# A decoder layer's two FFNs: where the combinations of x for the half-size products are made, and four plain blocks in the first FFN

## The chip, the cores and the metric

The kernel runs on one core of one Trainium2 chip. The metric is the device time of one execution in microseconds; the median of several runs is given. TensorE (PE) multiplies matrices, VectorE (DVE) and ScalarE (ACT) do elementwise work, GpSimd (POOL) a little of it, and SyncE's queue (SP) issues the loads of weights.

## The reference, cut to what matters

The input x is 512 tokens by 1024 features, float32. The layer is a SwiGLU FFN of half weight, a token mixer, and another FFN of half weight:

```python
x = x + 0.5 * swiglu(rmsnorm(x, ffn1_norm), ffn1_w_gate, ffn1_w_up, ffn1_w_down)
h = rmsnorm(x, mix_norm); proj = h @ w_in
...
x = x + jnp.concatenate([hm, hp], axis=-1) @ w_out
x = x + 0.5 * swiglu(rmsnorm(x, ffn2_norm), ffn2_w_gate, ffn2_w_up, ffn2_w_down)
return rmsnorm(x, final_norm)
```

with `swiglu(h, g, u, d) = (silu(h @ g) * (h @ u)) @ d` and an inner width of 2816, which is 22 blocks of 128 features. mlstm heads (`hm`) and a causal pooling (`hp`) stand in the mixer; they play no part here.

## The kernel before, in words

Everything lies transposed: features on the 128 partitions, the 512 tokens along the free axis. x is 8 tiles of 128 x 512 (k = 0 to 7). A float32 product is made of three passes: each operand is split into a high part (`_hi`, rounded, made by ScalarE) and a low part (`_lo`, operand minus high part, made by VectorE), and TensorE does hi*hi, hi*lo and lo*hi. The weights come in units of 128 x 1024, which SP loads into two slots `raw`; ScalarE and VectorE split them into four slots `w_hi`, `w_lo`. A slot of `raw` is free for the next load once its low part is made (`lo_made`).

An FFN (`ffn_up`) has 22 blocks of inner features. Each needs a gate column and an up column.

- A **plain block** uses two weight units, 24 matmuls of 512 tokens each (L341 to L343), with x times its gain in `plain_x`. Gate and up land in two banks of `ps`; VectorE multiplies the gate by `rinv` (`plain_gate`, L1266), ScalarE takes the silu (L797), VectorE multiplies (`plain_product`, L1271), ScalarE copies the high part to `act_hi` (`act_high`, L802), VectorE makes the low part (`act_low`, L1262).
- A **half-size block** computes the 2 x 2 block product (gate and up against the two halves of the tokens, with the two halves of the inner dimension) by seven products instead of eight, each of 12 matmuls of 256 tokens (`product`, L426 to L428), 84 in all. Its seven weight factors are sums of four 128 x 512 blocks, made by VectorE (`sum_1` L1231, `sum_3` L1237, `sum_2` L1241, `sum_4` L1248), then split by ScalarE (L793) and VectorE (L1256). The results are put together by ScalarE's copies of P1, P5 and U2 (L815, L819, L830) and VectorE's corners (L1277 to L1300). The products stand in the order 1, 5, 6, 2, 7 with 3 and 4 of the block before among them (`period`). Product 6 waits for the copy of P1.

The half-size products also need **combinations of x**: for each k below 4, from the tile k and the tile k+4, each cut in halves of 256 tokens, the four terms t1, t3, t2, t4 (`x_terms`: L1215, L1216, L1218, L1220). t1 is split into `xg_hi`/`xg_lo` (L772, L1222), the other three together into `xe_hi`/`xe_lo` (L774, L1225). ScalarE first copies tile k times its gain to `rinv`, used as scratch here (L769), and before all that the part of x that is used as it is (`own_block`, L780, L781). Product 1 of the first block waits for all of these (`te_made`).

`rinv`, the reciprocal root of the mean square of every token, spread over the partitions, is made thus: TensorE sums columns (`mean_columns`, L383), VectorE computes the root (`inverse_rms`, L1190 and L1178 to L1183), TensorE spreads it over the partitions (`replicate`, L375) at a fixed place in the matmuls of the fourth unit, VectorE copies it (`take_rinv`, L1199).

Before the change each FFN has 2 plain blocks (`PLAIN`) and then 20 half-size ones (`NS`). Every engine works a list in fixed order; what lies ahead in one's list delays all behind it. VectorE's list at the start of an FFN is:

```python
x_terms(0); x_terms(1); inverse_rms(stage); x_terms(2); x_terms(3)
sum_1(0); sum_3(0, True); sum_2(0); lo_of(1, 0, 0); lo_of(5, 0, 0)
take_rinv(stage); plain_gate(0); lo_of(6, 0, 0); sum_4(0, True); plain_product(0)
```

(one line each there). The first FFN follows the loading of x; the second follows the mixer's output projection (`out_blocks(WO_UNIT, 1, 2, ...)`), in which, for each of 8 columns d, TensorE does one unit, VectorE adds the result to x[d] (L1382), splits a weight unit (L1148), makes the low part of x[d] times its gain (L1154) and adds the square (L1164), and ScalarE splits a unit (L743), makes the high part (L753) and squares (L760).

Of the kernel before, what the change touches and what calls it, by code (L numbers as in the profile page):

```python
# [30 lines left out]
T = 512  # L31
# [18 lines left out]
PLAIN = 2  # L50
NS = FB - PLAIN
UPP1 = 0
DN1 = UPP1 + 2 * PLAIN
# [8 lines left out]
DN2 = UPP2 + 2 * PLAIN  # L62
N_UNITS = DN2 + DN_UNITS * KD
SUP = (N_UNITS, N_UNITS + 2 * NS)
AFTER = (DN1, DN2)
N_ROWS = N_UNITS + 4 * NS
# [32 lines left out]
def build_layer(nc, weights, pool_w, x_t, vecs, consts, out):  # L99
    ctx = ExitStack()  # L100
    with ctx:
# [51 lines left out]
        tt = work[:, 0:2].rearrange("p a n -> p (a n)")  # L153
# [5 lines left out]
        zeros = sums[:, 3]  # L159
# [101 lines left out]
        def _(sp):  # L261
# [28 lines left out]
            def strassen_blocks(p):  # L290
                q = AFTER[p]
                sp.wait_ge(lo_made, q - 1)
                load_block(p, 0, 0)
                load_block(p, 0, 1)
                sp.wait_ge(lo_made, q)
                load_block(p, 0, 2)
                load_block(p, 0, 3)
                with sp.Fori(1, NS) as s:
                    sp.wait_ge(s_made[3], s + p * NS)
                    load_block(p, s, 2)  # L300
                    sp.wait_ge(f_lo[1], s + p * NS)
                    load_block(p, s, 0)
                    sp.wait_ge(f_lo[4], s + p * NS)
                    load_block(p, s, 3)
                    sp.wait_ge(f_lo[2], s + p * NS)
                    load_block(p, s, 1)
                sp.wait_ge(f_lo[1], (p + 1) * NS)
                sp.wait_ge(f_lo[2], (p + 1) * NS)
                load(q, q)
                sp.wait_ge(s_made[3], (p + 1) * NS)  # L310
                sp.wait_ge(f_lo[4], (p + 1) * NS)
                load(q + 1, q + 1)
# [10 lines left out]

            strassen_blocks(0)
# [14 lines left out]
        def _(pe):  # L339
# [52 lines left out]
            def ffn_up(base, p, stage, mean_at, rep_at):  # L392

                def plain(f):
# [13 lines left out]
                    for i in range(2):  # L408
                        n = base + 2 * f + i
                        column_block(n, n, ps[:, 2 * f + i], before(2 * f + i), plain=True)  # L410
# [8 lines left out]
                def product(i, s, par, acc, first=False):  # L419

                    pe.wait_ge(f_lo[i], s + (p * NS + 1))
# [9 lines left out]
                def last_two(s, par, steps):  # L431

                    if 3 in steps:
                        pe.wait_ge(p5_copied, s + (p * NS + 1))
                        product(3, s, par, ps_c[par])
                    if 4 in steps:
                        pe.wait_ge(c22_made, s + (p * NS + 1))
                        product(4, s, par, ps_b[par])

                def period(s, par, early=False, head=False):  # L440
                    if head:
                        pe.wait_ge(b11_made, 2 * (p + 1))
                        pe.wait_ge(te_made, 2 * KH * (p + 1))
                    if not early:
                        pe.wait_ge(prod_made, s + (p * FB + PLAIN - 1))
                    product(1, s, par, ps_b[par], True)
                    if not early:
                        pe.wait_ge(c12_made, s + (p * NS - 1))
# [3 lines left out]
                    pe.wait_ge(p1_copied, s + (p * NS + 1))  # L452
# [5 lines left out]
                    else:  # L458
                        pe.wait_ge(c11_made, s + p * NS)
                    product(2, s, par, ps_a, True)  # L460
                    pe.wait_ge(u2_copied, s + (p * NS + 1))
                    product(7, s, par, ps_b[par])

                for f in range(PLAIN):
# [3 lines left out]
                with pe.Fori(1, NS // 2) as it:  # L468
                    period(it * 2, 0)
                    period(it * 2 + 1, 1)  # L470
                last_two(NS - 1, 1, (3, 4))
# [263 lines left out]
        def _(act):  # L735
# [25 lines left out]

            def ffn_up(base, p, stage):
                q = AFTER[p]

                def x_terms(k):

                    if k > 0:
                        act.wait_ge(t_step, 4 * (p * KH + k))
                    act.activation(rinv[:], x[:, k], ACT.Copy, scale=scalar_of(V_GAIN + stage * KD + k)  # L769
                                   ).then_inc(b1_made, 1)  # L770
                    act.wait_ge(t_step, 4 * (p * KH + k) + 1)
                    act.activation(xg_hi[:, k, HALF:T], tt[:, 0:HALF], ACT.Copy).then_inc(t_hi_made, 1)  # L772
                    act.wait_ge(t_step, 4 * (p * KH + k) + 4)
                    act.activation(xe_hi[:, :, k], tt[:, HALF:].rearrange("p (a n) -> p a n", n=HALF), ACT.Copy  # L774
                                   ).then_inc(t_hi_made, 1)

                def own_block():

                    act.wait_ge(xg_made, KD * stage + KH)
                    act.activation(xg_hi[:, 0:KH, 0:HALF], f32(act_hi[:, XP:FB, 0:HALF]), ACT.Copy).then_inc(b11_made, 1)  # L780
                    act.activation(xg_lo[:, 0:KH, 0:HALF], f32(act_lo[:, XP:FB, 0:HALF]), ACT.Copy).then_inc(b11_made, 1)  # L781

                def hi_of(i, s, par):

                    if i in (5, 6, 3, 7):
                        j = {5: 1, 6: 2, 7: 3, 3: 4}[i]
                        act.wait_ge(s_made[j], s + (p * NS + 1))
                        src = s_sum[j]
                    else:
                        j = {1: 0, 2: 1, 4: 3}[i]  # L790
                        act.wait_ge(blk_in[j], s * 16 + 16 * (p * NS + 1))
# [12 lines left out]
                def split_after(j):  # L804

                    for i in ((1, 5), (6, 2), (7, 3), (4,))[j]:
                        act.wait_ge(p_done[i], (p + 1) * NS)
# [4 lines left out]
                def iteration(s, par, head=False, tail=False):  # L812

                    act.wait_ge(p_done[1], s + (p * NS + 1))
# [3 lines left out]
                    act.wait_ge(p_done[5], s + (p * NS + 1))  # L818
# [7 lines left out]
                    else:  # L826
                        act.wait_ge(p_done[3], s + p * NS)
                    hi_of(3, s, par)
                    act.wait_ge(p_done[6], s + (p * NS + 1))
# [3 lines left out]
                    if not head:  # L833
                        silu(s + (PLAIN - 1))
                    if not tail:
                        if head:
                            act.wait_ge(unit_used, q)
                        else:
                            act.wait_ge(p_done[4], s + p * NS)
                        hi_of(4, s + 1, 1 - par)  # L840
                    if not head:
                        act_high(s + (PLAIN - 1))
                    if tail:
                        split_after(1)
                    else:
                        act.wait_ge(p_done[2], s + (p * NS + 1))
                        hi_of(2, s + 1, 1 - par)
                        act.wait_ge(p_done[7], s + (p * NS + 1))
# [8 lines left out]
                silu(0)  # L857
                act.wait_ge(unit_used, q - 2)
                hi_of(6, 0, 0)
                act_high(0)  # L860
# [3 lines left out]
                silu(1)  # L864
                act.wait_ge(unit_used, q)
                hi_of(4, 0, 0)
                act_high(1)
                iteration(0, 0, head=True)
                iteration(1, 1)
                with act.Fori(1, NS // 2 - 1) as it:  # L870
                    iteration(it * 2, 0)
                    iteration(it * 2 + 1, 1)
                iteration(NS - 2, 0)
                iteration(NS - 1, 1, tail=True)
# [5 lines left out]
            def out_blocks(base, per, stage):  # L880

                for d in range(KD):
# [8 lines left out]
                    square_x(d, stage)  # L891
                    if stage == 3:
# [252 lines left out]
        def _(dve):  # L1145
# [55 lines left out]

            def ffn_up(base, p, stage):
                q = AFTER[p]

                def x_terms(k):

                    at = 4 * (p * KH + k)
                    far = scalar_of(V_GAIN + stage * KD + KH + k)
                    b11, b12 = rinv[:, 0:HALF], rinv[:, HALF:T]
                    x21, x22 = x[:, KH + k, 0:HALF], x[:, KH + k, HALF:T]  # L1210
                    t1, t3, t2, t4 = (tt[:, i * HALF:(i + 1) * HALF] for i in range(4))
                    dve.wait_ge(b1_made, p * KH + k + 1)
                    if k > 0:
                        dve.wait_ge(te_made, 2 * (p * KH + k))
                    dve.tensor_tensor(t1, b12, b11, ALU.subtract).then_inc(t_step, 1)  # L1215
                    dve.scalar_tensor_tensor(t3, x22, far, b12, ALU.mult, ALU.subtract).then_inc(t_step, 1)  # L1216
                    dve.wait_ge(t_step, at + 2)
                    dve.tensor_tensor(t2, t3, b11, ALU.add).then_inc(t_step, 1)  # L1218
                    dve.wait_ge(t_step, at + 3)
                    dve.scalar_tensor_tensor(t4, x21, far, t2, ALU.mult, ALU.subtract).then_inc(t_step, 1)  # L1220
                    dve.wait_ge(t_hi_made, 2 * (p * KH + k) + 1)
# [534 lines left out]
```

## Time and profile before

| | |
|---|---|
| median of 3 runs | 958.43 us (958.25 to 959.22) |
| the profiled execution, device time | 960.42 us |
| its span in the trace | 958.6 us |
| mean granted TensorE clock | 0.976 of full |
| TensorE / VectorE / ScalarE / GpSimd busy | 95% / 73% / 48% / 6% |
| loaded from memory | 89.14 MB, 95 GB/s over the span |

The span is the trace's own clock from the first to the last instruction; the device time of the same execution is 1.8 us more. A busy share says little of what bounds a stage: an engine's row in the timeline names, in brackets, how long it idled before an instruction and what released it. Where a row is followed by the next start of the same engine, the difference is what the instruction costs in a full list; it can be less than its duration, since neighbours overlap a little.

### The profile page before, as it was taken

Reading aid. Unit: us, or ns where it says so; the run is one execution under the profiler, and the core shown is the slowest. Engines: PE = TensorE matmul, PEld = TensorE weight load, DVE = VectorE, ACT = ScalarE, POOL = GpSimd, SP = SyncE. Lnnn points to the kernel's source line nnn. Section 1 sums busy time; section 2 is a strip of 40 time slices with the busy share of each in tenths; the row PEclk is TensorE's granted clock in tenths of the full one; section 3 lists DMA queues with packets and bytes.
Section 4 is the critical chain, followed back from the end, with each engine's and each line's share of the span. In section 5 each row is a group of like instructions: output and inputs, shape, how many; then the busy total and the mean of one; then the engine's idle time right before and its main releaser. Section 6 shows DMA issues by size and latency. Waiting matters only on the chain.

```text
span 958.6 us, 15901 instructions
## 1 busy us (share of the span) xinstructions
PE 909.7 (95%) x5672; PEld 819.9 (86%) x5672; DVE 702.1 (73%) x1213; ACT 459.2 (48%) x766; POOL 58.2 (6%) x75
## 2 busy tenths in 40 slices
PE   8769999999999999999989999699999999999995
PEld 5569999999988888888878788599999999888885
DVE  7879999999744343578887676799999998534334
ACT  5455666666523232444772344556666665323220
POOL 4000000000000000000443300000000000000002
PEclk9879999999999999999999999799999999999997
DMA  5123332332343233222211131133323332432312
GB/s 187 61 84 98 106 108 92 109 109 91 107 143 102 97 109 110 75 81 86 67 67 44 66 114 62 44 111 109 109 89 108 109 98 99 132 102 99 107 44 88
DMA packets 40005, 91.73 MB, mean 96 GB/s; under 512 B 4401, under 2 KB 7729, under 8 KB 39969
## 3 DMA queue, kind: packets, MB, share of 16 engines
q1 hardware_dynamic: 39792, 90.79, 29.0%
q8 instruction: 22, 0.36, 0.2%
q0 software_dynamic: 176, 0.46, 0.1%
q14 instruction: 15, 0.11, 0.0%
HBM read 89.14 MB, written 2.10 MB: 95 GB/s over the span
## 4 chain that ended last, share of the span: by engine, by line
PE 42%; DVE 32%; DMA 12%; issue 8%; ACT 5%; DVEq 1%; SPq 0%; ACTq 0%
PE ps L341 14%; PE ps L342 14%; PE ps L343 13%; DMA raw<-weights 11%; DVE w_lo L1256 11%; DVE sums L1248 3%; DVE sums L1237 3%; DVE work L1280 3%; DVE work L1286 1%; DVE work L1288 1%; DVE work L1277 1%; ACT xe_hi L774 1%; DVE sums L1241 1%; ACT w_hi L743 1%; DVE xe_lo L1225 1%
## 5 line engine op out<-in xcount | busy, mean ns | idle before, releaser
L1148 DVE TENSOR_TENSOR w_lo<-raw,w_hi 128x1024 fp32r<-128x1024 f32 x83 | 103.6, 1249 | 127.5 <-ACT w_hi L743 121.3
L426 PE MATMUL ps<-xg_hi,w_hi 128*128 128x256 f32 x640 | 185.5, 290 | 5.1 <-DVE w_lo L1256 3.1
L341 PE MATMUL ps<-act_hi,w_hi 128*128 128x512 f32 (+1 forms) x470 | 180.7, 385 | 3.5 <-DVE act_lo L1154 3.0
L427 PE MATMUL ps<-xg_lo,w_hi 128*128 128x256 f32 x640 | 181.8, 284 | 0.0
L428 PE MATMUL ps<-xg_hi,w_lo 128*128 128x256 f32 x640 | 181.7, 284 | 0.0
L342 PE MATMUL ps<-act_lo,w_hi 128*128 128x512 f32 (+1 forms) x470 | 179.2, 381 | 0.0
L343 PE MATMUL ps<-act_hi,w_lo 128*128 128x512 f32 (+1 forms) x470 | 179.2, 381 | 0.0
L743 ACT ACTIVATE w_hi<-raw 128x1024 fp32r<-128x1024 f32 x75 | 79.2, 1057 | 179.9 <-PE ps L343 172.8
L426 PE MATMUL ps<-xe_hi,w_hi 128*128 128x256 f32 x480 | 136.5, 284 | 17.3 <-ACT work L815 15.7
L428 PE MATMUL ps<-xe_hi,w_lo 128*128 128x256 f32 x480 | 136.0, 283 | 0.0
L427 PE MATMUL ps<-xe_lo,w_hi 128*128 128x256 f32 x480 | 134.8, 281 | 0.0
L426 PEld LDWEIGHTS ps<-xg_hi,w_hi 128*128 128x128 f32 x640 | 123.0, 192 | 9.5 <-issue 5.9
L427 PEld LDWEIGHTS ps<-xg_lo,w_hi 128*128 128x128 f32 x640 | 123.3, 193 | 0.0
L428 PEld LDWEIGHTS ps<-xg_hi,w_lo 128*128 128x128 f32 x640 | 123.3, 193 | 0.0
L793 ACT ACTIVATE w_hi<-sums 128x512 fp32r<-128x512 f32 x160 | 97.1, 624 | 29.4 <-DVE sums L1231 28.2
L341 PEld LDWEIGHTS ps<-act_hi,w_hi 128*128 128x128 f32 x470 | 89.0, 189 | 23.6 <-DVE act_lo L1154 2.8
L1256 DVE TENSOR_TENSOR w_lo<-sums,w_hi 128x512 fp32r<-128x512 f32 x160 | 106.0, 683 | 2.4 <-ACT w_hi L793 2.4
L426 PEld LDWEIGHTS ps<-xe_hi,w_hi 128*128 128x128 f32 x480 | 91.7, 191 | 18.2 <-ACT work L815 16.2
L343 PEld LDWEIGHTS ps<-act_hi,w_lo 128*128 128x128 f32 x470 | 89.0, 189 | 17.0
L342 PEld LDWEIGHTS ps<-act_lo,w_hi 128*128 128x128 f32 x470 | 89.1, 190 | 16.1
L427 PEld LDWEIGHTS ps<-xe_lo,w_hi 128*128 128x128 f32 x480 | 91.8, 191 | 0.0
L428 PEld LDWEIGHTS ps<-xe_hi,w_lo 128*128 128x128 f32 x480 | 91.2, 190 | 0.0
(185 smaller groups left out, 1398.1 us busy)
## 6 DMA issues: line engine op xcount, KB each, us to landing
raw<-weights SPq DMA_DIRECT2D x82, 512.0 KB, 3.3
raw<-weights SPq DMA_DIRECT2D x160, 256.0 KB, 2.7
x<-x_t SPq DMA_DIRECT2D x8, 256.0 KB, 4.7
out<-x SPq DMA_DIRECT2D x6, 256.0 KB, 2.2
raw<-weights SPq DMA_DIRECT2D x9, 128.0 KB, 4.4
out<-x SPq DMA_DIRECT2D x4, 128.0 KB, 2.0
raw<-weights SPq DMA_DIRECT2D x1, 384.0 KB, 3.0
arena<-pool_w POOLq DMA_DIRECT2D x1, 256.0 KB, 4.2
```

Source lines behind the costliest of these rows:

```text
L341: pe.matmul(acc, hi, m_hi, start=first, stop=False)
L342: pe.matmul(acc, hi, m_lo, start=False, stop=False)
L343: return pe.matmul(acc, lo, m_hi, start=False, stop=last)
L426: pe.matmul(acc, hi[:, at], m_hi, start=first and k == 0, stop=False, skip_group_check=True)
L427: pe.matmul(acc, hi[:, at], m_lo, start=False, stop=False, skip_group_check=True)
L428: mm = pe.matmul(acc, lo[:, at], m_hi, start=False, stop=k == KH - 1, skip_group_check=True)
L743: act.activation(w_hi[:, k % SLOTS], raw[:, k % RAWS], ACT.Copy).then_inc(hi_made, 1)
L793: act.activation(factor(i, par, p)[0], src, ACT.Copy).then_inc(f_hi[i], 1)
L1148: dve.tensor_tensor(w_lo[:, k % SLOTS], raw[:, k % RAWS], f32(w_hi[:, k % SLOTS]), ALU.subtract).then_inc(lo_made, 1)
L1237: dve.tensor_tensor(s_sum[3], block_of(p, 0), block_of(p, 2), ALU.subtract).then_inc(s_made[3], 1)
L1248: dve.tensor_tensor(s_sum[4], block_of(p, 1), s_sum[2], ALU.subtract).then_inc(s_made[4], 1)
L1256: dve.tensor_tensor(lo, src, f32(hi), ALU.subtract).then_inc(f_lo[i], 1)
```

## The change

It does three things.

1. The scratch for the combinations moves: the scaled copy of tile k goes to `b1_sb` (a slice of `sums`) instead of `rinv`, and the terms to `tt` in `sums` instead of `work`. `x_terms` is cut in parts: `terms_first` and `terms_hi` on ScalarE, `terms` and `terms_lo` on VectorE.
2. The first FFN has 4 plain blocks and 18 half-size ones. The combinations of k = 0 to 3 stand among the splits, gates and products of the plain blocks. The last plain block's up column uses bank 1 again, so TensorE waits for the first block's product (`prod_made`); product 1 of the first half-size block waits for the product of the third plain block, and product 5 for the gate of the fourth, whose banks they take.
3. In the second FFN (still 2 plain and 20 half-size) the combinations are made in the output projection: for columns d = 4 to 7, behind the square, `terms(1, d - 4)`, and `terms_lo(1, d - 5)` from d = 5; the last `terms_lo(1, 3)` follows `inverse_rms`. `take_rinv` now stands before the first weight sum.

The weight units are laid out accordingly. SP loads units 4 to 7 before the first blocks. Semaphore counts with `p * NS` become `SB[p]`, and so on; these lines are left out.

```diff
-PLAIN = 2
-NS = FB - PLAIN
+PLAIN = (4, 2)
+NSP = (FB - PLAIN[0], FB - PLAIN[1])
+SB = (0, NSP[0])
...
+PLAIN_BANKS = ((0, 1), (2, 3), (4, 5), (6, 1))
...
+        b1_sb = sums[:, 1]
+        tt = sums[:, 2:4].rearrange("p a n -> p (a n)")
...
+            units(4, DN1)
             strassen_blocks(0)
...
+                        if f == 3 and i == 1:
+                            pe.wait_ge(prod_made, p * FB + 1)
+                        column_block(n, n, ps[:, PLAIN_BANKS[f][i]], before(2 * f + i), plain=True)
...
+                    if not early or PLAIN[p] == 4:
+                        pe.wait_ge(prod_made, s + (p * FB + PLAIN[p] - 1))
+                    product(1, s, par, ps_b[par], True)
+                    if head and PLAIN[p] == 4:
+                        pe.wait_ge(gate_scaled, p * FB + PLAIN[p])
...
-                own_block()
-                for k in range(KH):
-                    x_terms(k)
+                if p == 0:
+                    own_block(0)
+                    terms_first(0, 0)
+                    terms_hi(0, 0)
+                    terms_first(0, 1)
+                    split_hi(4, 4, 3)
+                    silu(0)
+                    terms_hi(0, 1)
+                    terms_first(0, 2)
+                    act_high(0)
+                    split_hi(5, 5, 3)
+                    silu(1)
+                    terms_hi(0, 2)
+                    terms_first(0, 3)
+                    act_high(1)
+                    split_hi(6, 6, 4)
+                    terms_hi(0, 3)
+                    split_hi(7, 7, 4)
+                else:
+                    terms_hi(1, 3)
...
+                    if stage == 2 and d >= KH:
+                        if d == KH:
+                            own_block(1)
+                        else:
+                            terms_hi(1, d - KH - 1)
+                        terms_first(1, d - KH)
...
-                x_terms(0)
-                x_terms(1)
-                inverse_rms(stage)
-                x_terms(2)
-                x_terms(3)
-                dve.wait_ge(unit_used, base + 1)
+                if p == 0:
+                    terms(0, 0)
+                    inverse_rms(stage)
+                    terms_lo(0, 0)
+                    terms(0, 1)
+                    take_rinv(stage)
+                    plain_gate(0)
+                    split_lo(4, 4)
+                    terms_lo(0, 1)
+                    plain_product(0)
+                    terms(0, 2)
+                    act_low(0)
+                    split_lo(5, 5)
+                    plain_gate(1)
+                    terms_lo(0, 2)
+                    plain_product(1)
+                    terms(0, 3)
+                    act_low(1)
+                    split_lo(6, 6)
+                    terms_lo(0, 3)
+                    split_lo(7, 7)
+                else:
+                    inverse_rms(stage)
+                    terms_lo(1, 3)
+                    take_rinv(stage)
+                f = PLAIN[p] - 2
...
+                    if stage == 2 and d >= KH:
+                        if d > KH:
+                            terms_lo(1, d - KH - 1)
+                        terms(1, d - KH)
```

## Rows read from the trace of the kernel before

**Rows 1.** The page, its first part: busy time (share of the span) and instructions of an engine.

```profile
PE 909.7 (95%) x5672; PEld 819.9 (86%) x5672; DVE 702.1 (73%) x1213; ACT 459.2 (48%) x766; POOL 58.2 (6%) x75
```

**Rows 2.** The list of waits: who waited for whom; us in total, times, longest.

```profile
PE ps L426 <- ACT work L815: 15.7, 2, 7.9
```

**Rows 3.** Timeline of TensorE, first FFN: start, us, engine, line, shapes, [idle before <- releaser].

```profile
36.09 2.07 PE L375 MATMUL ps<-ident,ycol 128*128 128x128 f32 x8 [5.25 <-DVE ycol L1183]
...
46.20 0.36 PE L426 MATMUL ps<-xg_hi,w_hi 128*128 128x256 f32 x1 [1.93 <-DVE w_lo L1256]
...
49.03 0.28 PE L428 MATMUL ps<-xg_hi,w_lo 128*128 128x256 f32 x1
57.18 0.58 PE L426 MATMUL ps<-xe_hi,w_hi 128*128 128x256 f32 x1 [7.87 <-ACT work L815]
...
62.25 0.41 PE L428 MATMUL ps<-xg_hi,w_lo 128*128 128x256 f32 x1
...
62.97 0.28 PE L426 MATMUL ps<-xe_hi,w_hi 128*128 128x256 f32 x1
```

**Rows 4.** Timeline of VectorE, first FFN.

```profile
26.19 0.42 DVE L1215 TENSOR_TENSOR work<-rinv 128x256 f32<-128x256 f32 x1 [0.92 <-ACT rinv L769]
...
27.91 0.42 DVE L1222 TENSOR_TENSOR xg_lo<-work,xg_hi 128x256 fp32r<-128x256 f32 x1
28.98 0.96 DVE L1225 TENSOR_TENSOR xe_lo<-work,xe_hi 128x768 fp32r<-128x768 f32 x1 [0.65 <-ACT xe_hi L774]
...
33.70 0.15 DVE L1190 TENSOR_SCALAR acol<-ps 128x4 f32<-128x4 f32 x1
...
36.07 0.42 DVE L1215 TENSOR_TENSOR work<-rinv 128x256 f32<-128x256 f32 x1
...
43.57 0.68 DVE L1231 TENSOR_TENSOR sums<-raw 128x512 f32<-128x512 f32 x1
...
46.58 0.68 DVE L1199 COPY rinv<-ps 128x512 f32<-128x512 f32 x1
47.30 0.69 DVE L1266 TENSOR_TENSOR work<-ps,rinv 128x512 f32<-128x512 f32 x1
...
68.09 0.69 DVE L1231 TENSOR_TENSOR sums<-raw 128x512 f32<-128x512 f32 x1 [1.01 <-DMA raw<-weights]
...
78.29 0.69 DVE L1231 TENSOR_TENSOR sums<-raw 128x512 f32<-128x512 f32 x1 [0.42 <-DMA raw<-weights]
...
240.91 0.69 DVE L1231 TENSOR_TENSOR sums<-raw 128x512 f32<-128x512 f32 x1 [0.32 <-DMA raw<-weights]
```

**Rows 5.** Timeline of VectorE, end of the output projection and second FFN.

```profile
576.94 0.69 DVE L1382 TENSOR_TENSOR x<-ps,x 128x512 f32<-128x512 f32 x1 [1.80 <-PE ps L343]
578.09 1.23 DVE L1148 TENSOR_TENSOR w_lo<-raw,w_hi 128x1024 fp32r<-128x1024 f32 x1 [0.46 <-ACT w_hi L743]
...
582.38 0.69 DVE L1382 TENSOR_TENSOR x<-ps,x 128x512 f32<-128x512 f32 x1 [1.80 <-PE ps L343]
...
604.56 0.69 DVE L1231 TENSOR_TENSOR sums<-raw 128x512 f32<-128x512 f32 x1
```

**Rows 6.** Timeline of TensorE, second FFN.

```profile
586.94 0.39 PE L341 MATMUL ps<-xg_hi,w_hi 128*128 128x512 f32 x1
...
600.81 1.05 PE L375 MATMUL ps<-ident,ycol 128*128 128x128 f32 x8
...
618.18 0.58 PE L426 MATMUL ps<-xe_hi,w_hi 128*128 128x256 f32 x1 [7.88 <-ACT work L815]
```

**Rows 7.** Timeline of ScalarE, first FFN.

```profile
25.45 0.71 ACT L769 ACTIVATE rinv<-x,vec 128x512 f32<-128x512 f32 x1
...
48.02 0.63 ACT L797 ACTIVATE work<-work 128x512 f32<-128x512 f32 x1 [3.10 <-DVE work L1266]
```

**Rows 8.** The weight loads of L287, 20 to 35 us, from issue to landing.

```profile
DMA to landing us min/median/max: 3.0/3.4/3.8
```

**Rows 9.** Windows, first FFN: us, busy of each engine (x), PEclk, DMA share, GB/s.

```profile
55.00:60.00 5.00, 2.82 (x13) 2.82 (x14) 2.27 (x4) 2.68 (x6) 0.00 (x0) 0.50 0.30 105
```

More of the change, by code:

```diff
@@ L443, in period @@
                         pe.wait_ge(te_made, 2 * KH * (p + 1))
+                    if not early or PLAIN[p] == 4:
[3 more added lines that the diff above has]
+                        pe.wait_ge(gate_scaled, p * FB + PLAIN[p])
                     if not early:
[L445 to L448, printed above, removed]
+                        pe.wait_ge(c12_made, s + (SB[p] - 1))
                     product(5, s, par, ps_c[par], True)
@@ L760, in square_x, with terms_first, terms_hi, own_block @@
                 act.activation(sq[n % 2], x[:, d], ACT.Square).then_inc(sq_made, 1)
+            def terms_first(p, k):
+                if k > 0:
+                    act.wait_ge(t_step, 4 * (p * KH + k))
+                act.activation(b1_sb, x[:, k], ACT.Copy, scale=scalar_of(V_GAIN + 2 * p * KD + k)).then_inc(b1_made, 1)
+            def terms_hi(p, k):
+                act.wait_ge(t_step, 4 * (p * KH + k) + 1)
+                act.activation(xg_hi[:, k, HALF:T], tt[:, 0:HALF], ACT.Copy).then_inc(t_hi_made, 1)
+                act.wait_ge(t_step, 4 * (p * KH + k) + 4)
+                act.activation(xe_hi[:, :, k], tt[:, HALF:].rearrange("p (a n) -> p a n", n=HALF), ACT.Copy
+                               ).then_inc(t_hi_made, 1)
+            def own_block(p):
+                act.wait_ge(xg_made, KD * 2 * p + KH)
+                act.activation(xg_hi[:, 0:KH, 0:HALF], f32(act_hi[:, XP:FB, 0:HALF]), ACT.Copy).then_inc(b11_made, 1)
+                act.activation(xg_lo[:, 0:KH, 0:HALF], f32(act_lo[:, XP:FB, 0:HALF]), ACT.Copy).then_inc(b11_made, 1)
             def ffn_up(base, p, stage):
                 q = AFTER[p]
[L765 to L781, printed above, removed]
                 def hi_of(i, s, par):
@@ L833, in iteration @@
                     if not head:
-                        silu(s + (PLAIN - 1))
+                        silu(s + (PLAIN[p] - 1))
                     if not tail:
@@ new lines, in terms_lo @@
+            def terms_lo(p, k):
+                dve.wait_ge(t_hi_made, 2 * (p * KH + k) + 1)
+                dve.tensor_tensor(xg_lo[:, k, HALF:T], tt[:, 0:HALF], f32(xg_hi[:, k, HALF:T]),
+                                  ALU.subtract).then_inc(te_made, 1)
+                dve.wait_ge(t_step, 4 * (p * KH + k) + 4)
+                dve.wait_ge(t_hi_made, 2 * (p * KH + k) + 2)
+                dve.tensor_tensor(xe_lo[:, :, k], tt[:, HALF:].rearrange("p (a n) -> p a n", n=HALF),
+                                  f32(xe_hi[:, :, k]), ALU.subtract).then_inc(te_made, 1)
@@ L1202, in ffn_up @@
             def ffn_up(base, p, stage):
                 q = AFTER[p]
[L1205 to L1221, printed above, removed]
-                    dve.tensor_tensor(xg_lo[:, k, HALF:T], t1, f32(xg_hi[:, k, HALF:T]), ALU.subtract).then_inc(te_made, 1)
-                    dve.wait_ge(t_step, at + 4)
-                    dve.wait_ge(t_hi_made, 2 * (p * KH + k) + 2)
-                    dve.tensor_tensor(xe_lo[:, :, k], tt[:, HALF:].rearrange("p (a n) -> p a n", n=HALF),
-                                      f32(xe_hi[:, :, k]), ALU.subtract).then_inc(te_made, 1)
@@ L1265, in plain_gate @@
                     dve.wait_ge(unit_used, base + 2 * f + 1)
-                    dve.tensor_tensor(g_full, ps[:, 2 * f], rinv[:], ALU.mult).then_inc(gate_scaled, 1)
+                    dve.tensor_tensor(g_full, ps[:, PLAIN_BANKS[f][0]], rinv[:], ALU.mult).then_inc(gate_scaled, 1)
                 def plain_product(f):
@@ L1703, in ffn @@
         down = down.transpose(0, 2, 1, 3).reshape(DN_UNITS * KD, P, UNIT)
-        return both[:2 * PLAIN], down, both[2 * PLAIN:]
+        return both[:2 * plain], down, both[2 * plain:]
     def mixer():
```

176 lines of the change are left out of this document (94 added, 82 removed).

## The prediction

> **What bounds the kernel now.** I read the page first: TensorE is busy 95% of the span [rows 1]. So only TensorE's holes, or its work, can give time. The list of waits names the largest single cause of holes: two waits of the product at L426 for ScalarE's copy at L815, 7.9 us each [rows 2]. The timeline of TensorE in the first FFN shows where they lie [rows 3]. In the middle of the fourth weight unit it idles 5.25 us, until 36.09, for the inverse root of the column means (L1183). It runs on, idles 1.93 us for the first low factor (L1256), does products 1 and 5 of the first half-size block from 46.20, and idles 7.87 us for the copy of P1. The first low factor and the copy of P1 are both late because VectorE is late: it makes the combinations of x alone, one k after another, from 26.19 to 43.57, and only then begins the weight sums [rows 4]. From the first weight sum to product 6 there are 57.18 - 43.57 = 13.61 us, a fixed ping-pong of sums, low parts, two plain gates, silus and copies between VectorE and ScalarE. In the second FFN the same chain ends in the same way (604.56 to 618.18, 13.62 us) [rows 5, 6]. After the restart a half-size block takes (240.91 - 78.29)/16 = 10.16 us [rows 4], for 84 matmuls. Products 1 and 5 (24 matmuls) took 46.20 to 49.15, 0.12 us each [rows 3], so 84 are 10.1 us: TensorE is full there, and VectorE nearly (it waits only 0.3 to 0.4 us a block, for a transfer).
>
> **First FFN: two half-size blocks go, two plain ones come, and the combinations lie under them.** I measure by the start of product 6 of the first half-size block, because everything behind it is the same code in the same order. Before it is at 57.18, with 20 blocks to do; after, 18. Two periods are worth 2 x 10.16 = 20.33 us. So the gain is 20.33 less the delay of that start.
>
> The delay follows from VectorE's new list. It begins at 26.19 as before, since ScalarE's first scaled copy of x (25.45, 0.71 us) stands behind the same two copies [rows 7]. Its pieces, mostly from starts of neighbouring instructions [rows 4]:
> - four combination groups, 27.91 - 26.19 = 1.72 each: 6.88
> - four pairs of low parts: the rows last 0.42 and 0.96; neighbours start 0.08 sooner than a row ends (five instructions of 0.68 from 43.57 to 46.58 are 0.60 each), so 0.34 + 0.88 = 1.22: 4.88
> - inverse root, 36.07 - 33.70: 2.37; copy of rinv, 47.30 - 46.58: 0.72
> - four new low parts of whole weight units, 1.23 - 0.08 = 1.15 [rows 5]: 4.60
> - for two plain blocks a gate, a product and a low part of the activation, six at 0.60: 3.60
> Sum 23.05. The waits for ScalarE I get by walking both lists side by side: ScalarE makes silu, xg_hi and xe_hi of the next k in this order, so VectorE waits 0.4 before xe_lo of k=1, 1.1 before xg_lo of k=2 (a silu of 0.63 [rows 7] and the small copy xg_hi stand before it), 0.4 before xe_lo of k=2, about 0.1 once more: 2.0. The old waits of 0.65 before each xe_lo go, since something else is done meanwhile. The last of the new low parts ends at 26.19 + 23.05 + 2.0 = 51.2. Only then may SP load blocks 2 and 3, two transfers of 256 KB; four such in a row at the same place landed after 3.0 to 3.8 us [rows 8]; I take 3.9 with issue and handover, as two follow each other. First weight sum: 55.1 (before, these blocks were in long before). From there the chain of 13.61, less the rinv copy that is made earlier (0.72), gives product 6 at 68.0. My walk of the old lists came out 0.4 early, which I add: 68.4. Delay 11.2, gain 20.3 - 11.2 = 9.1, taken as 9.0.
>
> TensorE hides in this. The inverse root is ready at 26.19 + 1.72 + 2.37 = 30.3, before TensorE asks at 36.09 - 5.25 = 30.8 [rows 3], so the 5.25 us go. A weight unit costs 582.38 - 576.94 = 5.44 us [rows 5]. Unit 4 is ready at 35.8 and TensorE comes at 35.7; unit 5 at 41.4 against 41.5; unit 6 at 48.9 against 47.0 (a 1.9 us hole); unit 7 ends near 59.9. Product 1 then waits for the third plain block's product (about 62.3, a hole of 2.4), product 5 for the gate of block 3, which sits in its bank (66.0, again 2.3), product 6 about 0.9. The new waits on prod_made and gate_scaled are on TensorE; behind them stand only products that the copy of P1 gates anyway, and that copy waits on ScalarE behind acthi of block 3, as before. The SP queue gets four loads of units more, each waiting for a low part made 8 us before its use.
>
> A rule speaks against plain blocks. By rows one costs 2 x 5.44 = 10.9 us of TensorE, one half-size block 10.16, so two swapped are +1.4 us of pure work; it is already in the sum, since the sum counts starts. The Trainium skill, "TensorE: Matmul & The Clock Gate", section "Wait — 56ns, not 53.3ns?", puts a back-to-back matmul at N/2.4 GHz plus about 2.5 ns. By that, an estimate, a half-size block would be 84 x 0.109 = 9.2 us, and the gain of this FFN about 2 us less. The rows differ (0.12), and they decide.
>
> **Second FFN: the combinations move into the output projection, columns 4 to 7.** There a unit takes TensorE 5.44 us and VectorE idles 1.80 + 0.46 = 2.26 of it [rows 5]. Added are 1.72 (column 4) and 1.72 + 1.22 = 2.94 (5 to 7) on VectorE. It falls behind by about 1.1 in column 4 (ScalarE's two copies of the own block, 1.9 us, stand before the first scaled copy), then 0.6 to 0.7 more each: 2.3 late at the last column, so x of the last column is made from 584.7 (582.38 + 2.3) and its low part, behind a w_lo of 1.15 and itself 0.74 long, ends at 587.2 (584.7 + 0.6 + 1.15 + 0.74). TensorE wants it at 586.94 [rows 6]: a hole of 0.3, the only price. The weight units split there are needed three units (16 us) later, and the mean's inverse root is ready at about 593, long before 601.
>
> What comes next: the list waits for the spread of rinv before the weight sums, and TensorE does that inside unit 3, at 600.81 + 0.3, ending 1.05 later [rows 6], at 602.1. rinv copied, the first weight sum starts at 602.85, against 604.56 [rows 5]: 1.7. The 0.72 of the rinv copy, before inside the chain, is now ahead of it. Gain 2.4. So most of the 16 us of combinations freed on VectorE turn into a wait for the spread, from 594.5 to 602.1; product 6 still waits, some 5.5 us in place of 7.88.
>
> **Sum.** 9.0 + 2.4 = 11.4 us. The profiled execution took 960.42 us (span 958.6 and 1.8 around it), so 949.0; it lies 2.0 over the median of the runs, 958.43, so the median becomes 947.0.
>
> **Bounds.** Transfers before the first sum: 3.0 at best, 5.2 if two of 2.6 don't overlap: +0.9, -1.3. Waits at handovers: 0 to twice 2.0. The second FFN: +2.7 without the hole; 0.5 if the lateness in the projection is doubled and TensorE waits 2 us for the last column. Everything else is priced by rows of the same instruction.
>
> **Rivals.**
> - The restart in the first FFN is 3 us later: the ScalarE handovers cost double. For it: two engines alternate over some 20 handovers, and ScalarE's stalls grow with VectorE's. Against: in the walk ScalarE works about 15 of the 25 us up to 51.2. 950.0, chance 0.12.
> - The second FFN gains nothing: VectorE's lateness in the projection holds up the first plain unit by 2 us or more. For it: 2.94 against 2.26 of idle. Against: the lateness cannot grow past column 7, and the last part is wanted 4.8 us after its column. 949.4, chance 0.09.
> - Better: handovers cost nothing and the transfers land in 3.0. 944.2, chance 0.07.
> - Slower: TensorE's clock stays at half over the restart. Before, the granted clock was 0.50 in 55 to 60 [rows 9] after the 7.87 us idle, and matmuls of 0.41 us until 62.25 instead of 0.28 at 62.97 [rows 3]; that cost nearly nothing, since the next period (68.09 to 78.29, 10.20) is at most 0.04 long [rows 4]. Now short runs of products stand between holes of 2.4, 2.3, 0.9 and 1.7 us. At half clock a block's 84 matmuls need about 0.21 us each, 7.7 us more a block; from some 1.5 blocks (11.4/7.7; 26 us) fully at half clock the gain is gone. Against: no stretch before was at half for more than about 6 us once TensorE ran again. 959 to 962, chance 0.03. The Trainium skill, same page, section "HAM oscillation — how this bites in real kernels", warns of idle gaps in TensorE's work throttling it; the trace agrees for 5.25 and 7.87 us, while the 1.93 us hole was followed by full speed.
> - That the change does nothing (within 0.2%, 1.9 us) needs both gains to fail: 0.01.
>
> **How the numbers follow.** My forecast has 0.68, at 947.0, own range 945.5 to 948.7. The range 944.5 to 950.6 takes in the first two rivals. A measurement of this kernel tells about 0.2% from no change; faster 0.96, same 0.01, slower 0.03.
>
> **What will show it.** In the first FFN: no wait before L375 there, TensorE near-solid to about 60, first weight sum at 54 to 56, product 6 at 67.5 to 69.5, and the down projection starting 9 us earlier. In the second: combinations in the last four columns of the projection, VectorE waiting about 7 us for the spread, the last wait for L815's successor 5 to 6 us. Wrong if product 6 starts after 71, if the period leaves 10.16, or if the projection's units exceed 5.44.

## The result

The changed kernel takes 946.76 us (median of 4 runs, 946.19 to 947.14), the kernel before 958.69 us in the same comparison: 11.9 us less, ratio 0.9875 (95% interval 0.9858 to 0.9892). Forecast were 947.0 us and 11.4 us less.

The profiled execution of the changed kernel took 946.77 us, its span is 945.0 us. TensorE in its first FFN, against [rows 3] (line numbers have moved: L345 is the plain matmul, L379 the spread, L432 the half-size one, L825 the copy of P1). These are all the rows between 28 and 75 us before which TensorE idled:

```profile
48.97 0.50 PE L345 MATMUL ps<-act_hi,w_hi 128*128 128x512 f32 x1 [1.68 <-DVE w_lo L1181]
...
62.09 0.35 PE L432 MATMUL ps<-xg_hi,w_hi 128*128 128x256 f32 x1 [1.93 <-DVE work L1308]
...
65.60 0.39 PE L432 MATMUL ps<-xg_hi,w_hi 128*128 128x256 f32 x1 [1.85 <-DVE work L1303]
...
67.92 0.38 PE L432 MATMUL ps<-xe_hi,w_hi 128*128 128x256 f32 x1 [0.62 <-ACT work L825]
...
72.58 0.39 PE L432 MATMUL ps<-xe_hi,w_hi 128*128 128x256 f32 x1 [1.55 <-ACT work L840]
```

The 5.25 us hole for the inverse root and the 7.87 us hole before product 6 are gone. Small ones stand in their place: 1.68, 1.93, 1.85, 0.62 us. Product 6 starts at 67.92 instead of 57.18, with 18 blocks to do instead of 20.

VectorE there, against [rows 4] (L1245: first combination of a k; L1223: start of the inverse root; L1232: copy of rinv; L1181: low part of a whole unit; L1268: first weight sum; L1255, L1259: low parts of combinations):

```profile
26.05 0.42 DVE L1245 TENSOR_TENSOR sums<-sums 128x256 f32<-128x256 f32 x1 [0.74 <-ACT sums L774]
...
27.77 0.15 DVE L1223 TENSOR_SCALAR acol<-ps 128x4 f32<-128x4 f32 x1
...
33.26 0.68 DVE L1232 COPY rinv<-ps 128x512 f32<-128x512 f32 x1
...
34.59 1.22 DVE L1181 TENSOR_TENSOR w_lo<-raw,w_hi 128x1024 fp32r<-128x1024 f32 x1
...
43.10 0.43 DVE L1255 TENSOR_TENSOR xg_lo<-sums,xg_hi 128x256 fp32r<-128x256 f32 x1 [1.00 <-ACT xg_hi L779]
43.91 0.96 DVE L1259 TENSOR_TENSOR xe_lo<-sums,xe_hi 128x768 fp32r<-128x768 f32 x1 [0.38 <-ACT xe_hi L781]
...
50.03 1.22 DVE L1181 TENSOR_TENSOR w_lo<-raw,w_hi 128x1024 fp32r<-128x1024 f32 x1
55.01 0.69 DVE L1268 TENSOR_TENSOR sums<-raw 128x512 f32<-128x512 f32 x1 [3.76 <-DMA raw<-weights]
...
78.71 0.69 DVE L1268 TENSOR_TENSOR sums<-raw 128x512 f32<-128x512 f32 x1 [0.95 <-DMA raw<-weights]
...
88.81 0.69 DVE L1268 TENSOR_TENSOR sums<-raw 128x512 f32<-128x512 f32 x1 [0.33 <-DMA raw<-weights]
...
231.27 0.69 DVE L1268 TENSOR_TENSOR sums<-raw 128x512 f32<-128x512 f32 x1 [0.39 <-DMA raw<-weights]
```

The list ends at 50.03 + 1.15 = 51.2, as walked (it began at 26.05, 0.14 us before the old one); the wait of 1.00 and the one of 0.38 before the low parts of k=2 are the foreseen ones; the first sum comes at 55.0. The steady period is (231.27 - 78.71)/15 = 10.17 us, as before.

The output projection and the second FFN, against [rows 5] (L1438: x plus the column's result; 554.96 is column 4, 573.70 column 7):

```profile
554.96 0.69 DVE L1438 TENSOR_TENSOR x<-ps,x 128x512 f32<-128x512 f32 x1 [1.80 <-PE ps L347]
...
561.48 0.69 DVE L1438 TENSOR_TENSOR x<-ps,x 128x512 f32<-128x512 f32 x1
...
567.59 0.69 DVE L1438 TENSOR_TENSOR x<-ps,x 128x512 f32<-128x512 f32 x1
...
573.70 0.68 DVE L1438 TENSOR_TENSOR x<-ps,x 128x512 f32<-128x512 f32 x1
...
591.33 0.69 DVE L1232 COPY rinv<-ps 128x512 f32<-128x512 f32 x1 [7.85 <-PE ps L379]
592.05 0.69 DVE L1268 TENSOR_TENSOR sums<-raw 128x512 f32<-128x512 f32 x1
```

Columns 4 to 7 follow 6.52, 6.11 and 6.11 us apart where TensorE needs 5.44, so VectorE is late by 6.52 + 6.11 + 6.11 - 3 x 5.44 = 2.4 us at the last. Then it has nothing to do for 7.85 us before the copy of rinv. TensorE, against [rows 6]:

```profile
576.23 0.50 PE L345 MATMUL ps<-xg_hi,w_hi 128*128 128x512 f32 x1 [0.23 <-DVE xg_lo L1187]
...
604.95 0.58 PE L432 MATMUL ps<-xe_hi,w_hi 128*128 128x256 f32 x1 [6.68 <-ACT work L825]
```

The last column costs TensorE a hole of 0.23 us; it is the only one between 555 and 598 us, so in the projection itself TensorE's units stayed at 5.44. Product 6 still waits, 6.68 us. Another hole of the kernel before, in front of product 1, is gone:

```profile
607.20 0.36 PE L426 MATMUL ps<-xg_hi,w_hi 128*128 128x256 f32 x1 [1.22 <-DVE w_lo L1256]
```

Three markers divide the time between the two traces. The first x of the first down projection is made 9.76 us earlier (277.47 before, 267.71 after). Column 4 of the output projection comes 11.10 us earlier (566.06, 554.96). Product 6 of the second FFN starts 13.23 us earlier [rows 6]. So the first FFN gave 9.8 and the second 2.1, together 11.9, the difference of the medians. The 1.3 us in between lie in the mixer, which the change doesn't touch; the last section says what goes with them. Behind product 6 of the second FFN the traces differ by another 0.4 (340.4 and 340.1 us to the end). For these two reasons the spans, 958.6 and 945.0, differ by 13.6 and the medians by 11.9.

### The profile page after: what moved, and what is told of

Read it like the earlier page. It is cut to its first block, busy times and chain, and to the rows that moved or that the text cites. A ratio compares the mean times of both kernels' runs of the same rounds, so it can differ in the third digit from the quotient of the medians.

```text
span 945.0 us, 15669 instructions
## 1 busy us (share of the span) xinstructions
PE 905.4 (96%) x5600; PEld 812.3 (86%) x5600; DVE 690.8 (73%) x1187; ACT 453.1 (48%) x750; POOL 58.2 (6%) x75
## 4 chain that ended last, share of the span: by engine, by line
PE 43%; DVE 33%; DMA 11%; issue 8%; ACT 4%; DVEq 1%; SPq 0%; ACTq 0%
PE ps L345 14%; PE ps L346 14%; PE ps L347 14%; DMA raw<-weights 11%; DVE w_lo L1293 11%; DVE sums L1285 3%; DVE sums L1274 3%; DVE work L1317 2%; DVE work L1323 1%; DVE work L1325 1%; DVE work L1314 1%; DVE w_lo L1181 1%; DVE sums L1278 1%; ACT w_hi L751 1%; DVE act_lo L1187 1%
## 5 line engine op out<-in xcount | busy, mean ns | idle before, releaser
L1181 DVE TENSOR_TENSOR w_lo<-raw,w_hi 128x1024 fp32r<-128x1024 f32 x87 | 108.4, 1247 | 126.4 <-ACT w_hi L751 120.2
L345 PE MATMUL ps<-act_hi,w_hi 128*128 128x512 f32 (+1 forms) x486 | 186.6, 384 | 5.1 <-DVE act_lo L1187 3.0
L432 PE MATMUL ps<-xg_hi,w_hi 128*128 128x256 f32 x608 | 175.8, 289 | 5.5 <-DVE work L1308 1.9
L433 PE MATMUL ps<-xg_lo,w_hi 128*128 128x256 f32 x608 | 172.4, 284 | 0.0
L434 PE MATMUL ps<-xg_hi,w_lo 128*128 128x256 f32 x608 | 172.4, 284 | 0.0
L432 PE MATMUL ps<-xe_hi,w_hi 128*128 128x256 f32 x456 | 129.3, 284 | 10.4 <-ACT work L825 7.3
L434 PE MATMUL ps<-xe_hi,w_lo 128*128 128x256 f32 x456 | 128.8, 282 | 0.0
L433 PE MATMUL ps<-xe_lo,w_hi 128*128 128x256 f32 x456 | 127.6, 280 | 0.0
L432 PEld LDWEIGHTS ps<-xg_hi,w_hi 128*128 128x128 f32 x608 | 116.5, 192 | 9.3 <-issue 5.3
L433 PEld LDWEIGHTS ps<-xg_lo,w_hi 128*128 128x128 f32 x608 | 116.8, 192 | 0.0
L434 PEld LDWEIGHTS ps<-xg_hi,w_lo 128*128 128x128 f32 x608 | 116.8, 192 | 0.0
L345 PEld LDWEIGHTS ps<-act_hi,w_hi 128*128 128x128 f32 x486 | 91.7, 189 | 26.4 <-DVE w_lo L1181 3.3
L432 PEld LDWEIGHTS ps<-xe_hi,w_hi 128*128 128x128 f32 x456 | 86.8, 190 | 11.4 <-ACT work L825 7.7
```

Of the source, the lines that this page charges most:

```text
L345: pe.matmul(acc, hi, m_hi, start=first, stop=False)
L432: pe.matmul(acc, hi[:, at], m_hi, start=first and k == 0, stop=False, skip_group_check=True)
L433: pe.matmul(acc, hi[:, at], m_lo, start=False, stop=False, skip_group_check=True)
L434: mm = pe.matmul(acc, lo[:, at], m_hi, start=False, stop=k == KH - 1, skip_group_check=True)
L1181: dve.tensor_tensor(w_lo[:, k % SLOTS], raw[:, k % RAWS], f32(w_hi[:, k % SLOTS]), ALU.subtract).then_inc(lo_made, 1)
```

## Experiments

All are timed against the kernel before on the same chip; its median was 958.68 us beside the first four and 959.9 us beside the last three. Differences to the changed kernel are to its median of 946.76 us, taken beside a kernel before of 958.69, so for the last three they may be up to 1.2 us too small; by the ratios these three are 7.5, 5.0 and 11.6 us under the changed kernel. Single traces also begin a little apart: VectorE's first combination is at 26.05 to 27.27 us, so where it matters below a start is also told from there.

**The first FFN's part alone.** Stages of the second FFN put back:

```diff
 # ScalarE, p == 1
-                    terms_hi(1, 3)
+                    own_block(1)
+                    for k in range(KH):
+                        terms_first(1, k)
+                        terms_hi(1, k)
 # VectorE, p == 1
-                    inverse_rms(stage); terms_lo(1, 3); take_rinv(stage)
+                    terms(1, 0); terms_lo(1, 0); terms(1, 1); terms_lo(1, 1)
+                    inverse_rms(stage)
+                    terms(1, 2); terms_lo(1, 2); terms(1, 3); terms_lo(1, 3)
 # take_rinv(1) behind lo_of(5, 0, 0); nothing of this in the output projection
```

> The first FFN as changed (4 plain blocks, combinations among them); the second FFN as before, with its combinations one after another behind the output projection and the rinv copy behind the first low factors. Theory (product 6 of each FFN's first half-size block sets the gain, 9.8 us in the first, 2.1 in the second): 2.1 us slower than the changed kernel, 948.9 us; the wait of product 6 in the second FFN is back at 7.9. Rival (the parts share a gain, the second FFN's is worth nothing by itself): 946.8.

Measured: 949.01 us (ratio 0.9894, 0.9879 to 0.9909). That is 2.2 us over the changed kernel where 2.1 was expected. Product 6 of the second FFN waits 7.87 us again:

```profile
607.10 0.58 PE L432 MATMUL ps<-xe_hi,w_hi 128*128 128x256 f32 x1 [7.87 <-ACT work L825]
```

From column 4 of the projection (554.98) to it there are 52.12 us, against 49.99 in the changed kernel: 2.13.

**The second FFN's part alone.** `PLAIN = (2, 2)`, the first FFN's lists as before, unit loads 4 to 7 in SP's list dropped.

> The second FFN as changed; the first with 2 plain blocks, 20 half-size ones and its combinations one after another ahead of them, as before. Theory: 9.8 us slower than the changed kernel, 956.6 us, and 2.1 faster than before. Rival (the combinations in the projection cost as much as they save): 958.7.

Measured: 955.82 us (0.9971, 0.996 to 0.9981), 2.9 us under the kernel before and 9.1 over the changed one; 2.1 and 9.8 were expected. By the ratio's interval the gain is 1.8 to 3.8 us, so the expected 2.1 is in it and the rival's zero is not. The trace has product 6 of the second FFN 49.98 us after column 4 (615.91 and 565.93), like the changed kernel. The parts add to within 0.6 us: alone they gave 9.7 and 2.9, together 11.9.

**Four plain blocks, combinations ahead of them.** The same instructions of VectorE and ScalarE in the first FFN in another order:

```diff
-                    terms(0, 0); inverse_rms(stage); terms_lo(0, 0); terms(0, 1); take_rinv(stage); ...
+                    terms(0, 0); terms_lo(0, 0); terms(0, 1); terms_lo(0, 1)
+                    inverse_rms(stage)
+                    terms(0, 2); terms_lo(0, 2); terms(0, 3); terms_lo(0, 3)
+                    take_rinv(stage); plain_gate(0); split_lo(4, 4); plain_product(0); act_low(0)
+                    split_lo(5, 5); plain_gate(1); plain_product(1); act_low(1); split_lo(6, 6); split_lo(7, 7)
```

> Changed kernel, but in the first FFN all combinations of x stand ahead of the splits, gates and products of the four plain blocks, on VectorE and ScalarE, as they stood before; still 4 plain and 18 half-size blocks. VectorE does the same instructions in another order. Theory (VectorE's list and the handovers set the restart; TensorE waits 5 us for the inverse root again and then for unit 4 until about 46): walked list by list, product 6 starts 5 to 6 us later than in the changed kernel, at 73 to 74.5; 952 to 953.5 us, so about half of the first FFN's gain stays with the swap of blocks alone. Rival 1 (the gain is the hiding of the combinations, the two swapped blocks only cost TensorE time): nearly all of 9.8 goes, 956 to 957. Rival 2 (the gain is the swap, the order is nothing): 946.8 to 948.

Measured: 952.07 us (0.9932, 0.9919 to 0.9946), 5.3 us over the changed kernel. Rows of TensorE with a hole before them, the first three and product 6 (L379 is the spread again):

```profile
36.47 2.07 PE L379 MATMUL ps<-ident,ycol 128*128 128x128 f32 x8 [5.51 <-DVE ycol L1211]
...
46.54 0.50 PE L345 MATMUL ps<-act_hi,w_hi 128*128 128x512 f32 x1 [2.09 <-DVE w_lo L1176]
...
71.28 0.38 PE L432 MATMUL ps<-xg_hi,w_hi 128*128 128x256 f32 x1 [1.25 <-DVE work L1298]
...
73.61 0.39 PE L432 MATMUL ps<-xe_hi,w_hi 128*128 128x256 f32 x1 [0.64 <-ACT work L825]
```

The hole for the inverse root is back (5.51), unit 4 comes at 46.54, product 6 at 73.61: 5.7 later than after the change, 5.2 counted from VectorE's first combination (26.58 here, 26.05 there). So the gain has two parts. Swapping two half-size blocks for plain ones is worth about 4 us even when nothing is hidden: 3.8 by the medians of this run and the one before it, which differ in the first FFN alone (955.82 - 952.07), and 4.2 by the starts of product 6 in those two traces (20.3 - (73.61 - 57.53)). It gains although it gives TensorE 1.4 us more work: before product 6 there is a hole of 0.64 us where there were 7.87. Hiding the combinations gives the other 5.3. Both rivals fall short alone.

**The copy of rinv late in the second FFN.**

```diff
                     inverse_rms(stage)
                     terms_lo(1, 3)
-                    take_rinv(stage)
...
                 lo_of(5, 0, 0)
+                if p == 1:
+                    take_rinv(stage)
                 plain_gate(f)
```

(with one wait of VectorE for its own last low part, which is over by then; the first two experiments have it too).

> Changed kernel, but in the second FFN the rinv copy stands behind the first weight sums and low factors, as before. VectorE, which idles 7.85 us before that copy in the changed kernel, then makes sums and factors in that time. Theory (the wait for the spread holds the weight sums): the first weight sum starts at about 583.5 in place of 592.05, the gate of the first plain block at 592.1 in place of 595.07, product 6 3.0 us earlier: 943.8 us. Rival (something else, the plain gates or TensorE, holds product 6): 946.8.

Measured: 943.31 us (0.984, 0.9827 to 0.9853), 3.4 under the changed kernel, 3.0 expected. VectorE:

```profile
584.20 0.68 DVE L1268 TENSOR_TENSOR sums<-raw 128x512 f32<-128x512 f32 x1
...
592.14 0.69 DVE L1232 COPY rinv<-ps 128x512 f32<-128x512 f32 x1 [4.84 <-PE ps L379]
592.87 0.69 DVE L1303 TENSOR_TENSOR work<-ps,rinv 128x512 f32<-128x512 f32 x1
```

The sums start at 584.20 and the wait for the spread is 4.84 us. Product 6 waits 3.68 us in place of 6.68, the expected 3.0.

**The spread one unit earlier, too.** `ffn_up(UPP2, 1, 2, (1, 2), (2, 2))` in place of `(3, 2)`, on top of the late copy.

> As the kernel with the late rinv copy, and TensorE spreads rinv in the third unit of the second FFN instead of the fourth, 5.4 us earlier (the root is ready at 582.2, the new place is at about 585). Theory (the two plain gates hang on the spread, then the chain to product 6 ends behind TensorE's own work): product 6 follows products 1 and 5 with a hole under 1 us, at about 598; 7.7 us faster than the changed kernel, 939.1 us. Rival (a fixed 13 us from the first sum or the last plain unit to product 6): 943.8, as with the late copy alone.

Measured: 939.65 us (0.9797, 0.9779 to 0.9815), 7.1 under the changed kernel, 7.7 expected. Product 6 comes 43.15 us after column 4 (556.22 and 599.37), 6.8 less than in the changed kernel. No hole is left before it; the first one after the spread is before product 7:

```profile
577.49 0.50 PE L345 MATMUL ps<-xg_hi,w_hi 128*128 128x512 f32 x1 [0.22 <-DVE xg_lo L1187]
...
586.05 1.05 PE L379 MATMUL ps<-ident,ycol 128*128 128x128 f32 x8
...
603.12 0.39 PE L432 MATMUL ps<-xe_hi,w_hi 128*128 128x256 f32 x1 [0.74 <-ACT work L840]
```

The gates come at once:

```profile
584.64 0.69 DVE L1268 TENSOR_TENSOR sums<-raw 128x512 f32<-128x512 f32 x1
...
587.65 0.68 DVE L1232 COPY rinv<-ps 128x512 f32<-128x512 f32 x1
588.37 0.69 DVE L1303 TENSOR_TENSOR work<-ps,rinv 128x512 f32<-128x512 f32 x1
```

**The first FFN's list reordered.** VectorE's list (ScalarE's accordingly):

```diff
                     terms(0, 3)
-                    act_low(1); split_lo(6, 6); terms_lo(0, 3); split_lo(7, 7)
+                    split_lo(6, 6); split_lo(7, 7); act_low(1); terms_lo(0, 3)
+                    plain_gate(2); plain_product(2)
                     sum_1(0); sum_3(0, True); sum_2(0); lo_of(1, 0, 0); lo_of(5, 0, 0)
-                    plain_gate(2); lo_of(6, 0, 0); sum_4(0, True); plain_product(2); lo_of(2, 0, 0); act_low(2)
+                    act_low(2); lo_of(6, 0, 0); sum_4(0, True); lo_of(2, 0, 0)
                     lo_of(7, 0, 0); plain_gate(3); plain_product(3); lo_of(4, 0, 0); act_low(3)
```

> Changed kernel, but in the first FFN the splits of units 6 and 7 go ahead of the last combinations' low parts, so that SP may load the first blocks 1.8 us earlier, and the gate, silu and product of the third plain block go ahead of the first weight sum, into VectorE's idle time before it (3.76 us). Theory (in the changed kernel product 6 waits on VectorE's list, not on TensorE): product 6 about 4.4 us earlier, at 63.5, TensorE's holes before it 2 us in all in place of 4.4, 942.4 us. Rival (the time is set by TensorE's units and the steady loop, which takes the gain back): 946.8.

Measured: 942.2 us (0.9823, 0.9807 to 0.9838), 4.6 under the changed kernel, 4.4 expected. VectorE waits 0.73 us before its first sum in place of 3.76, and product 6 starts 3.6 earlier:

```profile
50.59 0.68 DVE L1315 TENSOR_TENSOR act_lo<-work,act_hi 128x512 fp32r<-128x512 f32 x1
...
52.40 0.68 DVE L1319 TENSOR_TENSOR work<-ps,rinv 128x512 f32<-128x512 f32 x1
53.78 0.69 DVE L1324 TENSOR_TENSOR work<-ps,work 128x512 f32<-128x512 f32 x1 [0.70 <-ACT work L807]
55.20 0.69 DVE L1284 TENSOR_TENSOR sums<-raw 128x512 f32<-128x512 f32 x1 [0.73 <-DMA raw<-weights]
```
```profile
64.29 0.38 PE L432 MATMUL ps<-xe_hi,w_hi 128*128 128x256 f32 x1 [0.61 <-ACT work L825]
```

Weight unit 4, which stands ahead of anything the edit changes, begins at 37.06 in this execution and at 35.86 in the changed kernel's. With this difference of 1.2 between the two executions allowed for, the edit moved product 6 by about 3.6 + 1.2 = 4.8 us; by the bare starts it is 3.6. The 4.4 of the walk and the 4.6 of the medians lie between. VectorE's first combination is 1.2 later there too (27.27 and 26.05), and counted from it the first x of the down projection (264.55) comes 4.4 earlier.

**Both.** The last two edits together.

> The early spread with late rinv copy in the second FFN, and the reordered list in the first. Theory (the two heads are apart and add): 7.7 + 4.4 = 12.1 us under the changed kernel, 934.7 us. Rival (they share a bound): about 939.

Measured: 935.93 us (0.9754, 0.9738 to 0.977), 10.8 under the changed kernel and 24.0 under the kernel before beside it. The walk said 934.7; the two edits alone gave 7.1 and 4.6, 11.7 together, so they add but for 0.9 us, while the runs of this kernel spread over 1.7 (934.66 to 936.32). In the trace both heads are as in the single edits: product 6 comes 37.13 us after VectorE's first combination (37.02 with the reordered list alone, 41.87 in the changed kernel) and, in the second FFN, 43.16 after column 4 (43.15 with the early spread alone). This is the fastest version.

## Why the prediction was right

- **The measure.** All was reckoned at the start of product 6. Both parts alone, and the four single edits that move that start, came out within 1 us of what its displacement said. That what lies behind it doesn't change is borne out by the period, 10.16 and 10.17, and it can't be had finer than about 1 us from one trace: from product 6 to the first x of the down projection the seven traces with 18 blocks take 199.1 to 200.3 us, and from the second product 6 to the end all nine take 339.2 to 340.4.
- **VectorE's list** was forecast to end at 51.2 and does, 23.05 of work and 2.0 of waits. The first sum was forecast at 55.1, and is at 55.01; product 6 at 68.0 before a correction of 0.4 that I took over from the walk of the old list, and is at 67.92. So the correction was the term that was wrong: the walk of the new list needed none (VectorE's list began 0.14 earlier than taken, and product 6 came 0.08 earlier). The delay is then 67.92 - 57.18 = 10.7 and the gain 20.3 - 10.7 = 9.6; the last block's first sum says the same (240.91 - 231.27 = 9.6), the marker behind this FFN 9.8, where 9.0 was forecast.
- **TensorE's small holes** were forecast as 1.9, 2.4, 2.3 and 0.9, measured 1.68, 1.93, 1.85 and 0.62: right in place, each a little large.
- **The second FFN** gave 2.1 instead of 2.4. VectorE's lateness (2.3, measured 2.4) and the hole (0.3, measured 0.23) were right. The spread came later than forecast: VectorE's copy of rinv starts at 591.33 where 602.1 - 11.1 = 591.0 was forecast. The matmuls that need column 7 start 0.39 behind the old place (576.23 + 11.10 against 586.94), not 0.23, and the spread itself 0.53 (590.24 + 11.10 against 600.81), where the forecast took the 0.3 of the hole for the whole delay. Rows of full-speed matmuls last 0.39 us but start 0.23 apart; around a hole this overlap is missing, so a hole costs more than its own length.
- **The wait of product 6** there was forecast at 5.5 us, 5 to 6 as a sign, and is 6.68: the forecast took the whole gain off this wait and didn't count the 1.22 us hole before product 1, which went too. By this sign the forecast missed; the start of product 6, on which the sum rests, isn't touched by it.
- **The wait for the spread** as the thing that then holds the second FFN is shown: taken away in two steps, it gave 3.4 us and then 7.1 in all.
- **The rule on plain blocks.** The Trainium skill, "TensorE: Matmul & The Clock Gate", section "Wait — 56ns, not 53.3ns?", puts a back-to-back matmul at N/2.4 GHz plus about 2.5 ns; by an estimate from that page the first FFN's gain would have been about 2 us less. The trace doesn't agree for these matmuls: a period of 10.17 us for 84 of them is 0.121 us each, not 0.109, and the measured gain is 9.8.
- **The slower rival, TensorE's clock,** fell. In the windows of the changed kernel the column PEclk is the last but two:

```profile
58.00:62.00 4.00, 2.16 (x10) 1.46 (x8) 2.61 (x5) 1.29 (x3) 0.00 (x0) 1.00 0.32 97
62.00:66.00 4.00, 2.06 (x15) 1.89 (x16) 2.50 (x4) 1.96 (x4) 0.00 (x0) 1.00 0.02 6
66.00:70.00 4.00, 3.38 (x28) 3.17 (x28) 1.98 (x3) 2.43 (x6) 0.00 (x0) 1.00 0.30 103
...
600.00:605.00 5.00, 0.05 (x1) 0.05 (x1) 4.13 (x7) 2.72 (x7) 0.00 (x0) 0.58 0.00 0
605.00:610.00 5.00, 5.00 (x23) 5.00 (x24) 2.92 (x6) 2.54 (x7) 0.00 (x0) 0.50 0.30 107
610.00:615.00 5.00, 5.00 (x41) 5.00 (x40) 4.80 (x9) 2.67 (x6) 0.00 (x0) 0.90 0.46 154
```

In the first FFN nothing of half clock is left after the holes of 1.93, 1.85, 0.62 and 1.55 us. In the second, around the 6.68 us hole, the clock is at half (1.2 of 2.4 GHz): 0.58 on the mean from 600 to 605, 0.50 from 605 to 610.
- **What half clock costs** can be read at one place. After the 5.25 us hole of the kernel before, the same 8 matmuls of the spread and 18 of a unit ran as in the changed kernel without that hole. The last of them, in the kernel before and in the changed one:

```profile
43.89 0.39 PE L343 MATMUL ps<-xg_hi,w_lo 128*128 128x512 f32 x1
```
```profile
35.51 0.39 PE L347 MATMUL ps<-xg_hi,w_lo 128*128 128x512 f32 x1
```

From the start of the spread (36.09 and 30.73) it is 7.80 us before, at a granted clock of 0.50 from 36 to 42, and 4.78 after, at 1.00: 3.0 us of TensorE's time. They didn't set the time: TensorE then still waited 1.93 us for VectorE [rows 3]. The prediction reads the small cost at the restart from the period 68.09 to 78.29, but by then the clock was full again (1.00 from 63 on). The stretch that has the half clock in it is product 6 to the first sum of the third block: 10.91 us (57.18 to 68.09) with it, 10.79 (67.92 to 78.71) without. That it is small there is argued from these two; no run changes the clock alone.
- **What was luck.** The time came out within 0.3 us, closer than its parts: the first FFN gave 0.8 more than forecast, the second 0.3 less, and the kernel before was at 958.69 in the comparison, not 958.43. Two figures of the working are misread by little and carry nothing: the last part of x is wanted 586.94 - 582.38 = 4.6 us after its column, not 4.8, and the combinations take VectorE 4 x 3.85 = 15.4 us, not 16.

## What to carry to other kernels

When two engines feed a third through ordered lists, find the one instruction after which both versions run the same code, and walk the lists to its start from neighbouring rows; here that came within half a microsecond of the measured start in both FFNs, where busy shares said nothing. A faster algorithm (seven products for eight) pays only once its inputs are ready: plain blocks, dearer for the engine that multiplies, filled that wait here, for about 4 of the 9.8 us. And when preparation is moved ahead, look at what it next waits for: 7.85 us stood unused behind a spread whose place in the matmuls was unchanged, and the two edits at that place gave 7.1 us, where the move itself had given 2.1.

## What the runs showed of the hardware that was not expected

The mixer, the same code in all these kernels, takes one of two lengths. From the first x of the first down projection to column 4 of the output projection it is 288.6 us in the kernel before, with the second FFN's part alone, with the early spread (288.7) and in the last version (288.8), and 287.0 to 287.3 in the other five. In the long ones the granted clock of TensorE dips for a few microseconds at the same spot of the mixer, where it has several holes of 0.4 to 1.4 us. In the kernel before:

```profile
500.00:505.00 5.00, 4.30 (x19) 3.69 (x20) 4.49 (x18) 0.00 (x0) 1.51 (x2) 0.81 0.31 105
505.00:510.00 5.00, 5.00 (x30) 4.43 (x30) 2.99 (x4) 2.10 (x3) 0.00 (x0) 0.85 0.01 3
510.00:515.00 5.00, 5.00 (x30) 4.35 (x30) 2.97 (x11) 0.60 (x1) 0.00 (x0) 1.00 0.31 105
```

and in the changed kernel the same stretch, 10 us earlier, is at 1.00 throughout:

```profile
490.00:495.00 5.00, 4.00 (x22) 3.34 (x22) 4.48 (x18) 0.45 (x1) 1.95 (x3) 1.00 0.32 105
495.00:500.00 5.00, 5.00 (x36) 4.62 (x35) 3.94 (x5) 2.65 (x4) 0.00 (x0) 1.00 0.00 0
```

The long ones take 1.3 to 1.8 us more. It follows no edit (the early spread acts only behind it), so chance of the execution is the likeliest; that isn't shown, and what decides it was not tried. It may be part of why single executions of one kernel lie up to 3.4 us apart (956.96 to 960.36 for the kernel before, beside the last three experiments), and why a profiled execution is better compared stage by stage than by its span.
